# In a hybrid encoder's chunked scan, three vector steps go to GpSimd and one ScalarE step goes to VectorE

## The reference

```python
xdt = (x.astype(jnp.float32) * dt[..., None]).reshape(b, nc, q, g, hg, p)
...
y_diag = jnp.einsum('bctsg,bctsgh,bcsghp->bctghp', cb, decay_in, xdt)
decay_out = jnp.exp(acs[:, :, -1:] - acs)
states = jnp.einsum('bcsgn,bcsgh,bcsghp->bcghpn', bc, decay_out, xdt)
...
y_off = jnp.einsum('bctgn,bcghpn,bctgh->bctghp', cc, prev, jnp.exp(acs))
return (y_diag + y_off).reshape(b, s, g, hg, p)
...
y = y_fwd + y_bwd + d_skip.astype(jnp.float32).reshape(SSD_GROUPS, hg)[..., None] * xs
y = y.reshape(b, s, SSD_INNER) * jax.nn.silu(z.astype(jnp.float32))
```

## Time and profile before

| what | value |
|---|---|
| time, median of 3 runs (lowest to highest) | 2614.61 us (2613.61 to 2614.97) |
| span of the profiled execution, first to last instruction | 2612.3 us |
| busy: PE / DVE / ACT / POOL | 2557.5 / 1431.4 / 893.8 / 726.6 us |
| chain that ended last, by engine | PE 85%, DVE 8%, ACT 3%, issue 2%, DMA 1% |

### The profile page before, as it was taken

How to read it: one execution, slowest core, us unless ns; L and a number is a source line. 1 busy time by engine, 2 the same in 40 slices (tenths; PEclk the granted TensorE clock), 3 DMA queues, 4 the chain that set the end, 5 groups by cost and what they waited for, 6 DMA issues and landing times.

```text
span 2612.3 us, 33401 instructions
## 1 busy us (share of the span) xinstructions
PE 2557.5 (98%) x13362; PEld 2164.1 (83%) x13362; DVE 1431.4 (55%) x1687; ACT 893.8 (34%) x1540; POOL 726.6 (28%) x388
## 2 busy tenths in 40 slices
PE   7999999999999999999999999999999999999999
PEld 6989997788888888888788899887888888888887
DVE  3476559645444444444666755694564444444445
ACT  4335658413111222222234365683232222222221
POOL 3232110033333333333323311101333333333331
PEclk9999999999999999999999999998999999999999
DMA  4433443211111111111123344522111111111112
GB/s 152 129 121 122 150 135 131 77 49 49 49 49 49 49 49 49 49 49 49 62 97 97 97 145 146 161 91 76 54 49 49 49 49 49 49 45 45 48 48 74
DMA packets 72043, 204.64 MB, mean 78 GB/s; under 512 B 5816, under 2 KB 28344, under 8 KB 70456
## 3 DMA queue, kind: packets, MB, share of 16 engines
q1 hardware_dynamic: 51848, 178.13, 20.7%
q10 hardware_dynamic: 20056, 24.51, 3.1%
HBM read 175.32 MB, written 27.30 MB: 78 GB/s over the span
## 4 chain that ended last, share of the span: by engine, by line
PE 85%; DVE 8%; ACT 3%; issue 2%; DMA 1%; SPq 0%; ACTq 0%; DVEq 0%
PE PS L505 23%; PE PS L509 23%; PE PS L508 23%; PE PS L589 3%; PE PS L593 3%; PE PS L592 3%; PE PS L759 2%; PE PS L748 2%; DVE SEG L1847 1%; PE PS L738 1%; ACT LG L1246 1%; PE PS L737 1%; DVE CV L1644 1%; ACT PTX L1253 1%; DMA XTOK<-xtok 1%
## 5 line engine op out<-in xcount | busy, mean ns | idle before, releaser
L505 PE MATMUL PS<-HH,WH 128*128 128x512 f32 x1904 | 747.7, 393 | 0.0
L495 POOL CAST WH<-RAW 128x1024 fp32r<-128x1024 f32 x192 | 237.2, 1236 | 1828.9 <-PE PS L505 1368.2
L508 PE MATMUL PS<-HL,WH 128*128 128x512 f32 x1904 | 744.6, 391 | 0.0
L509 PE MATMUL PS<-HH,WL 128*128 128x512 f32 x1904 | 744.5, 391 | 0.0
L497 POOL TENSOR_TENSOR WL<-RAW,WH 128x1024 fp32r<-128x1024 f32 x192 | 494.6, 2576 | 15.4
L1915 DVE TENSOR_TENSOR X<-PS,X 128x512 f32<-128x512 f32 x384 | 259.0, 689 | 374.6 <-PE PS L509 374.3
L509 PEld LDWEIGHTS PS<-HH,WL 128*128 128x128 f32 x1904 | 357.4, 188 | 79.9
L505 PEld LDWEIGHTS PS<-HH,WH 128*128 128x128 f32 x1904 | 357.8, 188 | 77.9
L508 PEld LDWEIGHTS PS<-HL,WH 128*128 128x128 f32 x1904 | 357.7, 188 | 77.2
L1399 ACT ACTIVATE FPAD<-PS 128x512 f32<-128x512 f32 x176 | 102.5, 595 | 884.6 <-PE PS L509 884.6
L1933 DVE SCALAR_TENSOR_TENSOR CVV<-FPAD,PARM,CVV 128x1024 f32<-128x1024 f32 x44 | 95.3, 2165 | 377.8 <-ACT CVV L1405 377.8
(11 more groups left out here) (227 smaller groups left out, 3052.3 us busy)
## 6 DMA issues: line engine op xcount, KB each, us to landing
RAW<-wst SPq DMA_DIRECT2D x192, 512.0 KB, 3.5
TOE<-toe_d SPq DMA_DIRECT2D x64, 512.0 KB, 3.8
XBS<-xbc_d SPq DMA_DIRECT2D x24, 512.0 KB, 4.3
xbc_d<-CV ACTq DMA_DIRECT2D x16, 512.0 KB, 3.8
tok_d<-ST ACTq DMA_DIRECT2D x12, 512.0 KB, 3.5
ZG<-tok_d SPq DMA_DIRECT2D x16, 384.0 KB, 3.6
toe_d<-row_d SPq DMA_DIRECT2D x4, 1024.0 KB, 12.9
X<-xT SPq DMA_DIRECT2D x2, 2048.0 KB, 7.9
```

The costliest lines, as they stand in the source:

```text
L495: nc.gpsimd.tensor_copy(hi, raw).then_inc(hi_done, 1)
L505: ins = nc.tensor.matmul(out, wh, xh, start=first, stop=False)
L508: nc.tensor.matmul(out, wh, xl, start=False, stop=False)
L509: return nc.tensor.matmul(out, wl, xh, start=False, stop=last)
```

## The change

VectorE now scales the backward output (bank 6 into `Y2`), in one instruction of 512 columns, as the first step of a chunk; ScalarE's eight go. GpSimd takes four steps of every chunk: weighting x (`XW`), multiplying x by `d_skip` (`Y3`), and adding `Y2` and `Y1` to `Y3`. VectorE's last sum becomes `Y3` + bank 4, behind a new semaphore `y3_ready`. To make room for the scan on its list, GpSimd's one loop over all weight pieces is cut into pieces before and behind the scan of each layer. Nothing else moves.

```diff
+            def scan(l):
+
+                step = Steps(pool, p_step, SUM_STEPS)
+                step.begin(l)
+                for c in range(NT):
+                    n, xs = l * NT + c, by_head(XS[:, c % 2])
+                    pool.wait_ge(xs_ready, n + 1)
+                    if c < LINKS:
+                        if c:
+                            pool.wait_ge(sf_full, l * LINKS + c)
+                        nc.gpsimd.tensor_tensor(by_head(XW[:]), xs, per_head(WST[:, c, 0:8]), ALU.mult).then_inc(xw_ready, 1)
+                    pool.wait_ge(chunk_done, 1 + n)
+                    step.then(nc.gpsimd.tensor_tensor(by_head(Y3[:]), xs, per_head(par_("d_skip")), ALU.mult))
+                    if c < LINKS:
+                        pool.wait_ge(y2_ready, l * LINKS + c + 1)
+                        ins = nc.gpsimd.tensor_tensor(Y3[:], Y3[:], Y2[:], ALU.add)
+                        if c:
+                            step.then(ins)
+                    if c:
+                        pool.wait_ge(y12_done, 1 + l * LINKS + c)
+                        ins = nc.gpsimd.tensor_tensor(Y3[:], Y3[:], Y1[:], ALU.add)
+                    ins.then_inc(y3_ready, 1)
+                step.end()
+
+            for l in range(DEPTH):
+                u0 = l * UNITS
+                split_pairs(u0, u0 + IN_U + 1)
+                split(u0 + IN_U + 1, 0)
+                scan(l)
+                split(u0 + IN_U + 2, 1)
+                split_pairs(u0 + IN_U + 3, u0 + UNITS)
...
-                    if c < LINKS:
-                        act.wait_ge(yo_full, n + 1)
-                        act.wait_ge(chunk_done, 1 + n)
-                        for h in range(HEADS):
-                            cols = slice(h * HD, (h + 1) * HD)
-                            last = A(Y2[:, cols], PS[:, 6, cols], ACT.Copy, scale=EACS[:, c, 8 + h:9 + h])
-                        last.then_inc(y2_ready, 1)
...
-                        dve.wait_ge(xs_ready, n + 1)
+                        dve.wait_ge(yo_full, n + 1)
                         if c < LINKS:
-                            TT(by_head(XW[:]), by_head(XS[:, par]), heads(WST, 0), ALU.mult).then_inc(xw_ready, 1)
-                        dve.wait_ge(yo_full, n + 1)
+                            TT(by_head(Y2[:]), by_head(bank(6)), heads(EACS, 8), ALU.mult).then_inc(y2_ready, 1)
+                        if c:
+                            TT(by_head(Y1[:]), by_head(bank(5)), heads(EACS, 0), ALU.mult).then_inc(y12_done, 1)
                         if 0 < c < LINKS:
                             step.then(TT(by_head(CURF[:]), by_head(CURF[:]), heads(CDEC, 0), ALU.mult))
-                        if c:
-                            TT(by_head(Y1[:]), by_head(bank(5)), heads(EACS, 0), ALU.mult).then_inc(y12_done, 1)
...
-                        step.then(TT(by_head((Y3 if c else Y1)[:]), by_head(XS[:, par]), per_head(par_("d_skip")), ALU.mult))
...
-                        if c:
-                            dve.wait_ge(y12_done, 1 + k)
-                            step.then(TT(Y1[:], Y1[:], Y3[:], ALU.add))
-                        if c < LINKS:
-                            dve.wait_ge(y2_ready, k + 1)
-                            step.then(TT(Y1[:], Y1[:], Y2[:], ALU.add))
-
...
                         dve.wait_ge(yd_full, 2 + n + 1)
-                        TT(Y1[:], Y1[:], bank(4), ALU.add).then_inc(chunk_done, 1)
+                        dve.wait_ge(y3_ready, n + 1)
+                        TT(Y1[:], Y3[:], bank(4), ALU.add).then_inc(chunk_done, 1)
```

More of the change, by code:

```diff
@@ L53 @@
 LINKS = NT - 1
+SUM_STEPS = NT + LINKS - 1
 G_FIRST = 2 * KT
@@ L326, in trunk @@
         far_ready, ldt_ready = sem("far_ready"), sem("ldt_ready")
+        y3_ready, p_step = sem("y3_ready"), sem("p_step")
         exp_ready, w_masked, yo_full, sf_full = sem("exp_ready"), sem("w_masked"), sem("yo_full"), sem("sf_full")
@@ L482, in _, with split @@
             pool.sem_inc(w_ready, 2)
[L484 to L497, removed]
+            def split(u, s):
+                for hf in range(2):
+                    n = u * 2 + hf
+                    pool.wait_ge(raw_full[hf], 16 * (u + 1))
+                    if hf == 0:
+                        pool.wait_ge(w_used, u + 1)
+                    hi, lo = (t[:, W_AT[s] + hf * 4 * W_PITCH[s]:W_AT[s] + (hf + 1) * 4 * W_PITCH[s]]
+                              .rearrange("p (k n) -> p k n", k=4)[:, :, 0:UC] for t in (WH, WL))
+                    raw = RAW[:, hf, :].rearrange("p (k n) -> p k n", k=4)
+                    settle(pool)
+                    nc.gpsimd.tensor_copy(hi, raw).then_inc(hi_done, 1)
+                    pool.wait_ge(hi_done, n + 1)
+                    nc.gpsimd.tensor_tensor(lo, raw, hi.bitcast(F32), ALU.subtract).then_inc(w_ready, 1)
@@ new lines, in split_pairs, with by_head @@
+            def split_pairs(first, end):
+                with pool.Fori(first // SLOTS, end // SLOTS) as r:
+                    for s in range(SLOTS):
+                        split(r * SLOTS + s, s)
+            def by_head(t):
+                return t.rearrange("p (h e) -> p h e", h=HEADS)
+            def scan(l):
[20 more added lines that the diff above has]
+                step.end()
@@ L1826, in _ @@
                 dve.wait_ge(vr_ready, l + 1)
-                step = Steps(dve, chunk_step, 6 * NT - 4)
+                step = Steps(dve, chunk_step, 3 * NT - 2)
                 step.begin(l)
```

## The result

| kernel | median of 6 runs, us | lowest to highest |
|---|---|---|
| before | 2614.11 | 2612.95 to 2614.97 |
| changed | 2621.35 | 2620.73 to 2623.66 |

The ratio is 1.0031 (95% interval 1.002 to 1.0042): 7.2 us slower, where 14.6 was forecast. The profiled execution of the changed kernel took 2621.28 with a span of 2619.5.

What follows compares the result with a forecast made beforehand. VectorE was taken to bound the scan, at 9.25 us a middle chunk. A layer adds 0.5 + 5 x 1.35 + 0.35 - 0.3 = 7.3, two layers 14.6, on a median of 2614.6: 2629 us, range 2608 to 2644.

Steps and rivals of the forecast that it cites:

- What VectorE loses: Middle chunk: VectorE sheds 2.77 us (XW, d_skip product, two sums) and gains 0.61 for Y2, so 9.25 becomes 7.09.
- what the sums had covered: Middle chunk: VectorE now waits 0.64 us for L930 before its last sum and 0.23 more for L895.
- two SBUF inputs exclude GpSimd's steps: VectorE steps with two SBUF inputs can't overlap GpSimd's, about 1.1 us a block; steps with a PSUM input can.
- Which steps are blocked: Middle chunk: GpSimd blocks CURF's product (1.0 us), the first SEG step (0.5 to 0.6) and a second (1.0), together 2.6.
- First and last chunks: Per layer: chunk 0 +0.5 us with its gate's place unchanged, chunk 6 +0.35, chunk 7 -0.3.
- Sum: Whole run: 7.3 us a layer, 14.6 for two layers, giving 2629 us, 0.56% slower.
- `y3_ready` and ScalarE: In the scan: the new wait for y3_ready costs nothing, and relieving ScalarE of 1.8 us a chunk buys nothing.
- TensorE's floor of 8.7: Middle chunk: 8.7 us, read from chunk 1's 8.72, is the shortest that TensorE's list allows.
- the faster rival: TensorE bounds the scan, blocks are hidden: middle chunk 8.7, -5.4 us a layer, 2604 us; chance 0.13.
- The two cancel: Middle chunk 9.2 to 9.5 us, by shorter blocks or one falling into a wait: 2611 to 2618 us; chance 0.12.
- Far slower through a broadcast operand: GpSimd's scan steps block 2.1 us each: chunk 13.6, some 27 a layer, 2668 us; chance 0.06.
- The clock falls: TensorE drops to 1.2 GHz in one scan chunk of each layer, +6.8 us each: 2643 us; chance 0.03.

Runs made afterwards that it cites:

- experiment 1: Changed kernel with each of GpSimd's four scan steps replaced by three memsets, all waits kept: 2595.48 us, 0.9932 of the kernel before.
- experiment 2: Changed kernel with GpSimd's XW held until both masks of the chunk before are done: 2611.31 us, 0.9993 of the kernel before.
- experiment 3: Kernel before with only the d_skip product on GpSimd; its second kernel also moves Y1 ahead of XW on VectorE: 2601.72 us, 0.9953.
- experiment 9: Experiment 2's kernel with GpSimd's XW adding instead of multiplying and its first sum multiplying instead of adding: 2613.95 us, a single run.
- experiment 4: Kernel before with Y2 scaled on VectorE instead of ScalarE, nothing on GpSimd in the scan: 2618.97 us, 1.0022.
- experiment 5: Changed kernel with Y2 left on ScalarE, GpSimd keeping its four steps: 2606.96 us, 0.9976 of the kernel before.
- experiment 6: Against experiment 5, sums back on VectorE and Y1 ahead of CURF: 2601.19 us, 0.9954; the same with XW held back: 2601.88 us, 0.9958.
- experiment 7: Changed kernel with GpSimd's weighting of x (XW) done twice in every chunk: 2637.8 us, 1.0092 of the kernel before.
- experiment 3's first kernel: Kernel before with only the d_skip product on GpSimd, VectorE otherwise in its old order: 2609.58 us, 0.9984.

## Why the prediction was right about the sign and too large

- **What VectorE loses and what the sums had covered: right.** Forecast 7.09 + 0.64 + 0.23. The last sum starts 1.28 behind CURF's instead of 0.60, 0.68 more, and shows 0.60 idle; the first step starts 1.06 behind the last product instead of 0.84, 0.22 more (the 0.37 idle in its row holds the 0.15 that lay there before).
- **That two SBUF inputs exclude GpSimd's steps, and PSUM steps do not: right**, shown by experiments 1, 2 and 3. VectorE goes on a little before GpSimd's recorded end: 0.13 here (438.14 against 438.27), 0.19 by the prediction's own rows (611.05 against 611.24), not its 0.25. The Trainium skill (SBUF — State Buffer, "Who interferes with whom") says besides that a GpSimd instruction that only writes does not contend; experiment 1 agrees, with VectorE's steps at 0.68 and 0.69 under memsets.
- **Which steps are blocked: right, but for which of SEG's steps meets XW. The step that failed is the size of two blocks: 1.0 each for CURF and the second SEG step, measured 0.77 and 0.85** (first SEG 0.5 to 0.6, measured 0.62). The sum at 437.00 holds VectorE until 438.82 - 0.68 = 438.14, so 1.14, as forecast at 1.1, and it starts where it was forecast (1.93 behind the end of the chunk's opening sum, forecast 2.0); but VectorE came to CURF 0.2 later than the forecast assumed (2.30, forecast 2.1), because Y2 had just come 0.22 late from its wait for TensorE, and the wait was counted in the chain but not in the place of the block. XW's block is shorter than the sums': 1.04 alone against 1.27. Together 2.24 instead of 2.6, and 7.09 + 0.68 + 0.22 + 2.24 = 10.23 for a chunk that took 10.22.
- **First and last chunks: sign right, sizes off.** Chunk 6 lost 0.12, not 0.35: it has no XW block, and CURF's was 0.77 instead of 1.0 (SEG's, at 0.61, was near the forecast). Chunk 7 gained 0.80, not 0.3: one GpSimd step blocked one SEG product (0.69 to 1.64), the other fell under PSUM steps, and a wait of 0.56 that stood before Y1 there went (in the second layer the gain is 0.46). Chunk 0 lost 0.6 from its gate to its last sum (5.07 to 5.69 and 5.70), near the forecast 0.5. But the gate's place did not stay in the first layer. It came 0.4 sooner, which leaves a loss of 0.2 there: the prediction read its 0.90 as a wait for TensorE, while the row names no engine (issue) and TensorE's product before it, L906, had ended at 410.16.
- **Sum.** Forecast 7.3 a layer; measured 0.2 + 0.79 + 3.89 + 0.12 - 0.80 = 4.2 in the first and 0.57 + 3.98 = 4.6 in the second. Together that is 8.8, and the spans differ by 7.2. The missing 1.6 lies in places that the change leaves alone. Before the first scan the changed kernel is 1.95 ahead. Behind the scans a stretch at the lower clock falls on other work: in the first layer the changed kernel's first output products step by 0.43 us (from 491.86) where those before step by 0.23 (from 489.31; granted clock 0.74 against 1.00 from 490 to 500), which costs it 1.8; in the second layer it is the other way round and gives 1.6 back. No run shows that the change moves these stretches. The two rows below are the same early stretch before and after, with less of it at the lower clock. Among kernels with the same lists up to the scan the granted clock in it was 0.51 (exchanged operations, experiment 9) to 1.00 (experiment 1), so it is put down to the execution and not to the change; one trace of each kernel can't prove it.

```profile
50.60:57.50 6.90, 6.90 (x24) 4.49 (x23) 4.17 (x2) 0.00 (x0) 3.46 (x3) 0.51 0.00 1
```

```profile
50.60:57.50 6.90, 6.90 (x39) 5.76 (x38) 5.49 (x4) 0.39 (x1) 4.78 (x4) 0.75 0.04 7
```

- **`y3_ready` and ScalarE: right for the change** (the last sum waits for L973; experiment 4). The prediction said that ScalarE's relief brings the copy of x forward and keeps XW from being late; experiments 5 and 6, where XW is late, fit that. It did not see that XW would be cheaper late (experiment 2).
- **TensorE's floor of 8.7 was wrong**: 8.35 (experiment 1). The stretch that it was read from the earlier trace rows listed no wait at its ends but had some inside: the 16 matmuls of L930 took 2.25 in it and 1.89 in experiment 1. The forecast didn't rest on it; the faster rival did, and with 8.35 its own sum gives 7.6 a layer and 2599 instead of 2604.
- **Rivals.** *TensorE bounds*: not here, but it is what experiment 1 shows without blocks. *The two cancel*: experiment 2, with one of three blocks moved into a wait, as that rival had it. *Far slower through a broadcast operand*: wrong; with the broadcast table XW takes 1.04, less than the sums' 1.27. *The clock falls*: not in the change, where every chunk from 1 to 6 is at 1.00, but in experiment 7.

## What to carry to other kernels

Before giving VectorE's steps to GpSimd, write down for each which VectorE step stands beside it: one with two SBUF inputs stops until a GpSimd step that reads SBUF is nearly through, one that reads PSUM or a wait for another engine takes it for free. One well placed step (experiment 3) gained more than four (experiment 5), and the same step at another place (experiment 3's first kernel) lost nearly all of it. A blocked instruction looks busy, so compare the durations of the same step before and after, not the idle times.

## What was not expected of the hardware

- A GpSimd step of 128 x 512 takes 1.04 with one full tile of input (a broadcast table, or the same tile twice) and 1.27 to 1.28 with two different ones, where VectorE does not hold it up; multiplying and adding take the same. The prediction had feared the broadcast.
- In the scan TensorE's clock held at 1.00 in the change, at 8.95 busy of 10.22 a chunk. In experiment 7, where a chunk at 1.00 has 8.93 busy of 10.93, it fell for a stretch in six chunks, and there the delay of VectorE was paid a second time, 1.21 in the chunk shown.
